# Second block: products that begin before the norm's root is known, two panels chunk by chunk

## The reference

```
x = x + 0.5 * rms_norm(swiglu(rms_norm(x, pre[0]), ffn1), post[0])
h = rms_norm(x, pre[1])
mix = attention and a gated recurrence of h @ w_in, times w_out     (layer 0)
mix = (gate_b * short_conv(gate_c * xt)) @ w_out                    (layer 1)
x = x + rms_norm(mix, post[1])
x = x + 0.5 * rms_norm(swiglu(rms_norm(x, pre[2]), ffn2), post[2])
```

## Time and profile before

| | us |
|---|---|
| median of 3 runs | 4067.9 |
| lowest and highest of them | 4062.45, 4071.55 |
| the profiled execution's own time | 4060.82 |
| its span, first to last instruction | 4059.5 |
| TensorE matmuls busy | 3777.0 |
| VectorE busy | 1645.6 |
| ScalarE busy | 1174.4 |
| GpSimd busy | 192.7 |

### The profile page before, as it was taken

How to read it: one execution, slowest core, us unless ns; L and a number is a source line. 1 busy time by engine, 2 the same in 40 slices (tenths; PEclk the granted TensorE clock), 3 DMA queues, 4 the chain that set the end, 5 groups by cost and what they waited for, 6 DMA issues and landing times.

```text
span 4059.5 us, 46555 instructions
## 1 busy us (share of the span) xinstructions
PE 3777.0 (93%) x20036; PEld 3043.9 (75%) x20036; DVE 1645.6 (41%) x2083; ACT 1174.4 (29%) x1516; POOL 192.7 (5%) x150
## 2 busy tenths in 40 slices
PE   7989888999989878999899989889999999989997
PEld 5866677888878566788688867568876887777886
DVE  3125644222251475333433365543344334354334
ACT  3115232111132343322322244432233223333222
POOL 0000410000000121000000002000000000000000
PEclk9989799999989978999999999999999999999998
DMA  6414111111112101222222222012222222222222
GB/s 246 150 67 171 71 41 43 71 63 65 63 52 74 58 2 42 93 94 95 82 95 103 93 84 83 32 63 103 93 104 73 93 94 93 83 83 73 94 103 73
DMA packets 47643, 341.04 MB, mean 84 GB/s; under 512 B 5280, under 2 KB 5440, under 8 KB 7632
## 3 DMA queue, kind: packets, MB, share of 16 engines
q1 hardware_dynamic: 41184, 301.09, 20.8%
q0 software_dynamic: 5216, 34.88, 2.3%
q10 hardware_dynamic: 1040, 2.10, 0.1%
HBM read 335.95 MB, written 2.10 MB: 83 GB/s over the span
## 4 chain that ended last, share of the span: by engine, by line
PE 86%; DVE 7%; ACT 3%; issue 2%; POOL 2%; DMA 1%; DVEq 0%; POOLq 0%; ACTq 0%
PE PS L351 68%; PE PS L353 7%; PE PS L817 2%; DVE SQ L445 2%; PE PS L833 1%; POOL U L1339 1%; PE PS L392 1%; PE PS L872 1%; DVE nmax_a L967 1%; PE PS L1114 1%; DVE YS L1835 1%; PE PS L411 1%; DVE X L1842 1%; PE PS L504 1%; PE PS L403 1%
## 5 line engine op out<-in xcount | busy, mean ns | idle before, releaser
L328 DVE TENSOR_TENSOR WL<-raw,WH 128x2048 fp32r<-128x2048 f32 x260 | 595.8, 2292 | 413.4 <-ACT WH L323 413.4
L323 ACT ACTIVATE WH<-raw 128x2048 fp32r<-128x2048 f32 x260 | 495.4, 1905 | 461.9 <-PE PS L351 346.6
L351 PE MATMUL PS<-XH_ff,WH 128*128 128x512 f32 x704 | 278.8, 396 | 12.5 <-DVE XL_ff L456 12.5
L351 PE MATMUL PS<-XH_b,WH 128*128 128x512 f32 x704 | 276.9, 393 | 11.8 <-DVE XL_b L456 10.5
L351 PE MATMUL PS<-XH_a,WH 128*128 128x512 f32 x704 | 277.3, 394 | 11.1 <-DVE XL_a L456 9.7
L351 PE MATMUL PS<-XL_ff,WH 128*128 128x512 f32 x704 | 276.7, 393 | 0.0
L351 PE MATMUL PS<-XH_ff,WL 128*128 128x512 f32 x704 | 276.4, 393 | 0.0
L351 PE MATMUL PS<-XL_a,WH 128*128 128x512 f32 x704 | 275.6, 391 | 0.0
L351 PE MATMUL PS<-XH_a,WL 128*128 128x512 f32 x704 | 275.4, 391 | 0.0
L351 PE MATMUL PS<-XL_b,WH 128*128 128x512 f32 x704 | 275.3, 391 | 0.0
L351 PE MATMUL PS<-XH_b,WL 128*128 128x512 f32 x704 | 275.1, 391 | 0.0
(11 more groups left out here) (348 smaller groups left out, 7554.7 us busy)
## 6 DMA issues: line engine op xcount, KB each, us to landing
raw<-in_panels SPq DMA_DIRECT2D x260, 1024.0 KB, 4.8
ada_at<-in_ada_panels SPq DMA_DIRECT2D x24, 1024.0 KB, 4.8
ada_win<-in_ada_panels POOLq DMA_DIRECT2D x18, 1024.0 KB, 5.1
ada_start<-in_ada_panels POOLq DMA_DIRECT2D x6, 1024.0 KB, 22.8
FX<-in_dft_x POOLq DMA_DIRECT2D x2, 2048.0 KB, 8.0
X<-in_xT SPq DMA_DIRECT2D x1, 3072.0 KB, 11.4
out<-X ACTq DMA_DIRECT2D x1, 2048.0 KB, 6.9
rope<-in_rope POOLq DMA_DIRECT2D x2, 768.0 KB, 10.6
```

The costliest lines, as they stand in the source:

```text
L323: H.up(ac.activation(WH[s].rearrange("p k n -> p (k n)"), raw[:, s, :], ACT.Copy), n)
L328: L.up(ve.tensor_tensor(WL[s].rearrange("p k n -> p (k n)"), raw[:, s, :], WH[s].bitcast(F32).rearrange("p k n -> p (k n)"), ALU.subtract), n)
L351: t = te.matmul(PS[:, j, :], lhsT, x[:, k, 0:SEQ], start=st, stop=end)
```

## The change

- Panels have four places for WH and WL from the last "down" of the first block on (slot_of; in the middle of in0 and in the attention only two, since other buffers lie there). Splits follow a list made by split_steps: up to three panels ahead, at most two beside one panel, and none beside the first panel of a "wide" stage. Wide are the first "up" of each FFN, in{l} and out{l}. For a wide FFN or in-projection that starts at panel p0 this gives: panels p0 to p0+2 before the stage, none beside p0, p0+3 beside p0+1, p0+4 and p0+5 beside p0+2, p0+6 beside p0+3, then one each. In in0 none stands beside panels 3 and 4 (p0+3 and p0+4). Panel 139, the second of out0, is split at the start of the attention, and 140 beside out0's second panel (139).
- te_wide makes the first four products (two panels) chunk by chunk, in banks 0 to 3; product 4 goes to bank 4, product 5 to bank 7, later ones to banks 0 and 1 in turn.
- XH and XL are made of x times the norm's weights, without the root. Squares are added on VectorE beside them; TensorE's sum over chunks (L392) and GpSimd's half of XL are gone. The root's first part follows the four products, its spread follows product 4, and the result is copied to RN (which is YS[0]).
- Products are multiplied by RN where they leave PSUM: in an FFN VectorE now takes the gate ("gated"), ScalarE makes the silu in GA, VectorE multiplies by RN ("gate"), then by the up product ("hidden"). In in{l} VectorE evacuates in place of ScalarE.
- out{l} is wide too, but its input needs no root.
- The work beside in0 moves 5 products later. The output goes out in eight transfers, each behind its chunk.

```diff
@@ slots, the list of splits
+def slot_of(n):
+    if n < FOUR or FIRST["in0"] + 4 <= n < FIRST["out0"]:
+        return n % 2
+    return (n - FIRST["in0"]) % 4 if n < FIRST["out0"] else (n - FIRST["out0"]) % 4
...
+        while n < N_PANELS and n <= i + (3 if i >= FOUR else 1) and len(at[i]) < 2:
+            if earlier_of(n) is not None and earlier_of(n) >= last:
+                break
+            if n == FIRST["out0"] + 1 or (i in wide and n > i + 1):
+                break
+            at[i].append(n)
+            n += 1
+        if i == FIRST["out0"] - 1:
+            at["mo"] = [n]
+            n += 1
...
+def place(m):
+    return {4: 4, 5: 7}.get(m, m if m < 4 else m % 2)
@@ te_wide
+        def te_wide(name, n, XH, XL, ready, evac, beside=None, root=None):
+            p0 = FIRST[name]
+            def step(m, k):
+                s, j = slot_of(p0 + m // 2), m % 2
+                for q, (w, x) in enumerate(((WH, XH), (WH, XL), (WL, XH))):
+                    t = te.matmul(PS[:, place(m), :], w[s][:, k, j * P:(j + 1) * P], x[:, k, :],
+                                  start=k == 0 and q == 0, stop=k == NC - 1 and q == 2)
...
+            for k in range(NC):
+                ready(k)
+                for m in range(4):
+                    if k == 0:
+                        te.wait_ge(*L[p0 + m // 2])
+                        wait_bank(m)
+                    step(m, k)
+            if root:
+                te_root(root, False)
+            for m in range(4, 2 * n):
+                te.wait_ge(*L[p0 + m // 2])
+                if beside:
+                    beside(m)
+                wait_bank(place(m))
+                for k in range(NC):
+                    step(m, k)
+                if m == 4 and root:
+                    te_spread_root(root, False)
@@ ac_gemm (ve_gemm alike)
-                if FIRST[name] + p + 1 < N_PANELS:
-                    ac_split(FIRST[name] + p + 1)
+                for q in SPLITS[FIRST[name] + p]:
+                    ac_split(q)
@@ the entry
+        def ac_enter(name, before, ended_stage, XH, g):
+            ac_stats(before, False, False)
+            fence(ac, ended_stage)
+            for c in range(NC):
+                ac.wait_ge(*V[(name, "x", c)])
+                A.up(ac.activation(XH[:, c, :], X[:, c, 0:SEQ], ACT.Identity, scale=col("pre", g * NC + c)),
+                     (name, "XH", c))
+                if c >= 3:
+                    ac.wait_ge(*V[(name, "square", c - 2, "added")])
+                A.up(ac.activation((SQ[c % 2] if c else SS)[:, 0:SEQ], X[:, c, 0:SEQ], ACT.Square), (name, "square", c))
+            ac_stats(name, False, False, RN)
+        def ve_enter(name, before, ended_stage, XH, XL, g, start, x):
+            ve_stats(before, False)
...
+            def low(c):
+                ve.wait_ge(*A[(name, "XH", c)])
+                V.up(ve.scalar_tensor_tensor(XL[:, c, :], X[:, c, 0:SEQ], col("pre", g * NC + c),
+                                             XH[:, c, :].bitcast(F32), ALU.mult, ALU.subtract), (name, "XL", c))
+                if c:
+                    ve_square_sum(name, (name, "square", c), c % 2, SEQ, c == 1)
+            start(0)
+            for c in range(NC):
+                if c + 1 < NC:
+                    start(c + 1)
+                x(c)
+                if c:
+                    low(c - 1)
+            low(NC - 1)
+            ve_stats(name, False)
@@ ve_ffn2, up
+                    acc = PS[:, place(m) if g == 0 else j, :]
+                    ve.wait_ge(*B[(up, m)])
+                    if j == 0:
+                        ve.wait_ge(*V.now())
+                        V.up(ve.tensor_tensor(GA, acc, RN[:], ALU.mult), (up, "gated", c))
+                        ve.wait_ge(*A[(up, "silu", c)])
+                        V.up(ve.tensor_tensor(GA, GA, RN[:], ALU.mult), (up, "gate", c))
+                    else:
+                        ve.wait_ge(*V[(up, "gate", c)])
+                        V.up(ve.tensor_tensor(GA, acc, GA, ALU.mult), (up, "hidden", c))
+                        ve.wait_ge(*A[(up, "HH", c)])
@@ te_ffn2, what frees a bank
+                    bank(to, V, up, "gated" if m % 2 == 0 else "hidden", m // 2)
@@ ve_in2
+                ve.wait_ge(*B[(name, m)])
+                V.up(ve.tensor_tensor(b["U"][:, chunk_of(l, m), :], PS[:, place(m), :], RN[:], ALU.mult), (name, "u", m))
@@ te_beside_in (ac_ and ve_ moved by 5 as well)
-            if 3 <= m < 7:
-                c = m - 3
+            if 8 <= m < 12:
+                c = m - 8
@@ ac_moba (ve_moba alike)
+            for q in SPLITS["mo"]:
+                ac_split(q)
@@ ac_end
-            out_landed.up(ac.dma_start(out, X[:, :, 0:SEQ]), "out")
+            for c in range(NC):
+                ac.wait_ge(*V[("end", "x", c)])
+                out_landed.up(ac.dma_start(out[:, c, :], X[:, c, 0:SEQ]), "out")
```

More of the change, by code:

```diff
@@ L163, in program @@
     RS = keep.take("RS", [P, TOK])
+    for s in (2, 3):
+        top = Shelf(base + 219 * 1024 - 256 - (4 - s) * 2 * 4 * PANEL)
+        WH.append(top.take(f"WH{s}", [P, NC, 2 * P], F32R))
+        WL.append(top.take(f"WL{s}", [P, NC, 2 * P], F32R))
     eps = keep.take("eps", [P, 1])
@@ L265, in program @@
             b["sq"] = shelf.take("sq_", [P, 4])
+            shelf = Shelf(base + 219 * 1024 - 256 - 4 * 4 * PANEL)
+            for k in "ria":
+                b["lru_" + k] = shelf.take(f"lru_{k}", [P, 4, SEQ])
+            b["VT"] = shelf.take("VT2", [P, SEQ // P, 4 * P])
         mix2.append(b)
@@ L414, in te_stats, with ac_stats @@
             bank(6, A, name, "RS")
-            bank(7, A, name, "RS")
-        def ac_stats(name, ctx, summed):
+            if ctx:
+                bank(7, A, name, "RS")
+        def ac_stats(name, ctx, summed, into=RS):
             n = TOK if ctx else SEQ
@@ L468, in ac_normed @@
                 A.up(t, (name, "XH", c))
[L470 to L474, removed]
         def te_normed(name, shift):
@@ L1817, in ac_post @@
[L1817 to L1832, removed]
+        RN = YS[0]
@@ L1847, in gp_ffn2 @@
[L1847 to L1870, removed]
+                                             ALU.mult, ALU.mult), (name, "start", c))
+            def x(c):
+                ve.wait_ge(*V[(name, "start", c)])
+                V.up(ve.tensor_tensor(X[:, c, 0:SEQ], X[:, c, 0:SEQ], YS[c % 2][:], ALU.add), (name, "x", c))
+            return start, x
+        def ve_halve(g):
+            V.up(ve.tensor_scalar(col("post", g * NC, NC), col("post", g * NC, NC), 0.5, None, ALU.mult))
@@ new lines, in ac_square_sum, with te_ffn2, evac_up, evac_down @@
+        def ac_square_sum(name, m, src):
+            if m >= 3:
+                ac.wait_ge(*V[(name, "square", m - 2, "added")])
+            A.up(ac.activation((SQ[m % 2] if m else SS)[:, 0:SEQ], src, ACT.Square), (name, "square", m))
+        def te_ffn2(name, before):
+            b = ffn[name]
+            te_enter(before)
+            for g, nk in enumerate(GROUPS):
+                up, down = f"{name}.up{g}", f"{name}.down{g}"
+                def evac_up(m, to):
+                    bank(to, V, up, "gated" if m % 2 == 0 else "hidden", m // 2)
+                def evac_down(m, to):
+                    bank(to, V, down, "x", m)
@@ L1871, in evac_down @@
                 if g == 0:
-                    V.up(ve.tensor_copy(Y[:, m, :], PS[:, j, :]), (down, "x", m))
+                    te_wide(up, nk, b["XH"], b["XL"], te_entered(name), evac_up, None, name)
                 else:
[L1874 to L1877, removed]
```

274 lines of the change are left out of this document (162 added, 112 removed).

## The result

The changed kernel takes 4028.6 us in the median (4024.4 to 4032.9, 4 runs) against 4067.4 us (4062.5 to 4071.6) of the kernel before: a ratio of 0.9908, 95% interval 0.9889 to 0.9927. That is 38.8 us less; 37 were forecast. The profiled execution took 4031.1 us, its span is 4029.8 us.

What follows compares the result with a forecast made beforehand. TensorE is busy 93% of the span; only six gaps ahead of stages and the end can give time. FFNs 13.3, in1 15.3, in0 to out0 4.75 and end 3.7 sum to 37 us: 4031 against 4067.9, range 3965 to 4054.

Steps and rivals of the forecast that it cites:

- a0: FFN entry without an add before it: debt falls from 23.7 to 20.4 us, 3.3 us gained.
- b0, a1, b1: The three other FFN entries: debt falls from 25.75 to 22.4 us, 3.35 us gained at each.
- in1: In-projection entry: 25.75 us less 8.7 of new debt and 1.8 of wait at product 8, 15.3 us gained.
- in0: In-projection entry: 26.1 us less 8.7 of new debt and 2.75 of waits, 14.65 us gained.
- head of the attention: Panel 139's split moved there: mask starts 6.2 us after the last in-projection product, not 1.8; 4.4 us lost.
- out0: Starts with two panels split: panel 140 ready 4.4 us late, with 1.1 us of clock, 5.5 us lost.
- end: Output transfers: the last, of 256 KB, takes 3.2 us where one of 2048 KB took 6.9; 3.7 us gained.
- The entry: Chunk phase: first XL after 4.2 us, 2.2 us low clock, 2.2 us root groups; new debt 8.7 us.
- The evacuation: Each FFN entry: TensorE waits 3.35 us for panel 3's WL and 7.05 us for bank 0, 10.4 us together.
- Rival 1: FFN and in-projection entries: evacuation keeps up without those waits, 96 us gained, 3971 us; chance 0.20.
- Rival 2: Chunk phases at six boundaries: low clock stays, 96 matmuls take 41 us instead of 24, 4133 us; chance 0.05.
- Rival 3: FFN entries: each wait is 9 us longer, so nothing is gained, 4067 us; chance 0.05.

Runs made afterwards that it cites:

- e7: Changed kernel with eleven extra matmuls, whose result nothing reads, ahead of each entry's first chunk; 4018.8 us, ratio 0.9860.
- e4: Changed kernel with only the first panel's two products made chunk by chunk and the root right after them; 3994.5 us, ratio 0.9826.
- e1: Changed kernel with panel p0+3 of FFNs and in-projections split inside the entry, before the second root; 4017.3 us, ratio 0.9870.
- e2: Changed kernel with products going round six banks in each FFN's first up and in in1; 3995.0 us, ratio 0.9824.
- e3: Changed kernel with both panel p0+3 split inside the entry and six banks in the first ups and in1; 3971.9 us, ratio 0.9765.
- e6: Changed kernel with out0 made as before and panel 139 split beside its first panel; 4019.3 us, ratio 0.9859.
- e9: Changed kernel with panel p0+3 split in the entry, six banks, out0 as before, and eleven extra matmuls before each first chunk; 3951.5 us, ratio 0.9718.
- e5: Changed kernel with the output sent in one 2048 KB transfer behind the last x, as before; 4036.4 us in one execution.
- e8: Changed kernel with panel p0+3 split in the entry, six banks in the first ups and in1, and out0 as before; 3964.7 us, ratio 0.9723.

## Why the prediction was right

**The sum.** By its own steps, gained in us, forecast and measured in the profiled pair:

| | forecast | measured |
|---|---|---|
| a0 | 3.3 | 3.2 |
| b0, a1, b1 | 10.05 | 14.8 (5.55, 5.7, 3.55) |
| in1 | 15.3 | 16.6 |
| in0 | 14.65 | 15.3 |
| head of the attention | -4.4 | -4.4 |
| out0 | -5.5 | -6.1 |
| end | 3.7 | 4.9 |

They add up to 44.3, 2.2 us more than the 42.1 found. What is missing went back ahead of VectorE's start on x, in the root of the old norm, which no step of the sum held. From the last matmul of the stage before (at a0, from the start of the first block's last x) to that start it was 5.9, 5.8, 6.3 and 5.7 us at a0, in0, a1 and in1, and is 7.5, 6.3, 6.7 and 6.7: 3.3 us lost, of which other stretches gave 1.1 back. The small matmuls of that root are what is longer, as the chains before and after show at a0:

```profile
1989.93 1.37 PE PS L411 x8
...
2003.06 2.06 PE PS L506 x8
```

That the change causes this is not shown: in its second execution the kernel before takes 2.06 us for them too, and 7.4 us from that x to VectorE's start.

The steps were right one by one, but that the total is so near (37 forecast, 38.8 measured) is in part luck: the steps brought 7.3 us more than forecast, and 5.5 us were lost in places that the sum doesn't have, 2.2 in these roots, 2.2 in the first block (below) and 1.1 that nothing here resolves.

**The entry** was as written: first XL 4.1 us after VectorE's start, 96 matmuls in 23.4 to 24.9 us. e7 shows that the 1.6 to 3.1 us above 21.8 (2.2 in the mean, as forecast) are the clock after idle, all but 0.3 us, and e4 that VectorE, not TensorE, would pace a single panel. The root's two groups take 1.7 us, not 2.2; with fewer slow matmuls than counted (23.36 us) that is most of what in1 brought beyond its forecast.

**The evacuation** was the deciding step: without it the forecast would have been a gain of 96 us. The wait for WL of panel 3 was forecast at 3.35 and is 3.47 us, and e1 removes it by moving that split alone. The wait for bank 0 was forecast at 7.05 and is 4.1 to 5.3 us; e2 removes it by the bank alone. Here a term was mis-sized: I counted 1.1 us of low clock behind the first wait beside the 7.05 us. Products 6 and 7 take 1.9 us more than their 10.9 at b0 and a1, and 3.0 to 3.1 us more at b1 and a0. But that delays product 8's question, and it waits that much less: low clock and second wait add up to 7.16 us at all four places, where the sum had 8.15. Low clock that falls ahead of another wait is free. At b0, a1 and b1 that is 3.0 of the 4.7 us by which I was low, and the shorter root is 1.5. b1 came out lower (3.55 us) because its chunk phase took 24.86 us and the products behind the second wait 2.6 us too long, both by low clock.

**Rival 1** (3971 us) fell on the waits, and e3 shows what it stood for: with both waits gone the kernel is at 3971.9 us. **Rival 2** fell on the length of the chunk phases, 23.4 to 24.9 us and not 41. The sign that I gave for it, a clock below 0.9 over the 96 matmuls, was badly set: it is 0.88 at a0 and b1, since the eleven slow matmuls of my own sum already bring it to about 0.9. The Trainium skill's rule on bursts at the lower clock ("TensorE: Matmul & The Clock Gate", section "HAM oscillation — how this bites in real kernels") holds at one end here: after the wait of 4.89 us at a1 the first six matmuls are slow, while in e4 single waits of 1.05 to 1.08 us between chunks are followed by matmuls at the full rate. After the wait of 3.47 us at a1 the fall comes late: three matmuls go at the full rate, and the slow ones follow them. **Rival 3** did not occur.

**The end** was mis-sized by 1.2 us: a 256 KB transfer lands in 2.0 us (the page of the profile, above), not 3.2 by a line through two larger ones. The Trainium skill's "DMA: Bandwidth & Descriptors", section "Anatomy of one DMA — SWDGE (gpsimd) path", from which the prediction took its estimate of 2.6, gives its figures for transfers that GpSimd issues; this one is issued by ScalarE and was quicker.

**What I missed** is in the last "down" of the first block, whose first two panels now carry two splits each. Two WL in a row hold up the evacuation there, and TensorE waits 1.7 us for X (1.3 at most at once); with that stage's start at +10.15 us and its end at +12.4 us between the two profiles, it cost 2.2 us. In the waits of the changed kernel:

```profile
PE PS L404 <- DVE X L1744: 1.7, 2, 1.3
```

Its second execution shows the same 1.7 us, and neither execution of the kernel before has such a wait; no run moved these splits away. I had looked at the splits only from the panels' side, not from that of the evacuation that stands behind them. 42.1 less 2.2 is 39.9 us; the median's gain of 38.8, whose interval is 30 to 45 us, can't tell the 1.1 us between them.

## What to carry to other kernels

When work is moved off the path into the evacuation, write down when each bank comes free again, with everything that the evacuating engine has in front of it: here two choices (which bank product 8 gets, where one split stands) decided 50.7 us, more than the 42.1 that the change itself brought. An idle engine before a late scalar is the place for work that needs neither, and eleven matmuls without a use in a wait of 5 us gave back about 2 us at each of six places.

## What was not expected of the hardware

TensorE ran the same 512- and 256-column matmuls of the first block's first FFN, at granted clock 1.00 in both, at 579 in 100 us in the profiled executions of before, e4, e6 and e9, and at 567 to 568 in those of the changed kernel (twice), of e1, e3, e5, e7, e8 and of before again (569 in e2): 0.1727 or 0.1761 us each. It held over the whole FFN and made about 10 us; the second block's stages of 512 columns alone ran at one rate in all of them (266 or 267 in 60 us). Which of the two an execution gets wasn't found out. It is a quarter of the change's whole effect, and reason enough to compare stages and not only totals.
